# The last FFN by seven half products per pair of weight tiles (Strassen), with weight sums through PSUM and lo blocks split between VectorE and GpSimd

## The reference

```
def swiglu(h, w_in, w_out):
    gate, up = jnp.split(h @ w_in, 2, axis=-1)
    return (jax.nn.silu(gate) * up) @ w_out
# second_block, i = 1:
h = modulate(rmsnorm(x, norm_ffn_g[i]), sh2, sc2)
x = x + g2[:, None, :] * swiglu(h, w_ffn_in[i], w_ffn_out[i])
```

## Time and profile before

| | |
|---|---|
| median of three runs | 1659.35 us (1657.75 to 1660.1) |
| span of the profiled execution | 1656.0 us |
| TensorE busy in the span | 1628.9 us, 98% |
| VectorE, ScalarE, GpSimd busy | 804.0, 578.8, 734.7 us |
| last FFN (1281.5 to 1643 us) | 361.5 us |

### The profile page before, as it was taken

How to read it: one execution, slowest core, us unless ns; L and a number is a source line. 1 busy time by engine, 2 the same in 40 slices (tenths; PEclk the granted TensorE clock), 3 DMA queues, 4 the chain that set the end, 5 groups by cost and what they waited for, 6 DMA issues and landing times.

```text
span 1656.0 us, 21027 instructions
## 1 busy us (share of the span) xinstructions
PE 1628.9 (98%) x7254; PEld 1324.1 (80%) x7254; DVE 804.0 (49%) x1262; ACT 578.8 (35%) x790; POOL 734.7 (44%) x348
## 2 busy tenths in 40 slices
PE   8999999999999999999999999999999999999998
PEld 6785777878888888888888888888888888888886
DVE  6899887878565343433365161451725311111114
ACT  6434434344443322312244233232333431222233
POOL 5999133443244444444444334333424444444442
PEclk9999999999999999999999999999999999999999
DMA  9351266375455565555443223222213232222221
GB/s 383 119 208 65 90 239 212 115 263 206 179 204 190 203 253 192 199 195 187 159 148 107 69 89 101 67 85 78 98 52 96 82 101 94 96 99 92 95 74 61
DMA packets 65442, 233.71 MB, mean 141 GB/s; under 512 B 7264, under 2 KB 7264, under 8 KB 65120
## 3 DMA queue, kind: packets, MB, share of 16 engines
q1 hardware_dynamic: 65376, 232.82, 40.4%
HBM read 230.69 MB, written 2.10 MB: 141 GB/s over the span
## 4 chain that ended last, share of the span: by engine, by line
issue 55%; POOL 30%; PE 8%; DVE 3%; DMA 1%; ACT 1%; POOLq 1%; DVEq 0%; ACTq 0%
POOL w_lo L484 25%; POOL cv_acc L532 2%; PE bank L1542 2%; PE bank L1543 2%; PE bank L1544 2%; DVE mods_ring L1066 1%; POOL cv_y L514 1%; POOL diag L526 1%; POOL sq L526 1%; DVE x L1108 0%; DMA w_raw<-pl_v_in 0%; ACT sq L585 0%; DMA mods_ring<-w_mods_in 0%; PE bank L1573 0%; PE bank L1577 0%
## 5 line engine op out<-in xcount | busy, mean ns | idle before, releaser
L484 POOL TENSOR_TENSOR w_lo<-w_raw,w_hi 128x1024 fp32r<-128x1024 f32 x268 | 644.7, 2411 | 875.3 <-ACT w_hi L576 864.6
L1542 PE MATMUL bank<-h_hi,w_hi 128*128 128x512 f32 x1240 | 485.4, 391 | 1.2 <-POOL h_lo L496 0.9
L1544 PE MATMUL bank<-h_hi,w_lo 128*128 128x512 f32 x1240 | 482.7, 389 | 0.0
L1543 PE MATMUL bank<-h_lo,w_hi 128*128 128x512 f32 x1240 | 482.6, 389 | 0.0
L576 ACT ACTIVATE w_hi<-w_raw 128x1024 fp32r<-128x1024 f32 x264 | 277.8, 1052 | 261.1 <-PE bank L1544 242.8
L1542 PEld LDWEIGHTS bank<-h_hi,w_hi 128*128 128x128 f32 x1240 | 232.8, 188 | 51.7 <-issue 2.5
L1543 PEld LDWEIGHTS bank<-h_lo,w_hi 128*128 128x128 f32 x1240 | 232.8, 188 | 49.3 <-issue 1.2
L1544 PEld LDWEIGHTS bank<-h_hi,w_lo 128*128 128x128 f32 x1240 | 232.8, 188 | 48.5
L1542 PE MATMUL bank<-f_hi,w_hi 128*128 128x512 f32 x472 | 184.7, 391 | 0.9 <-DVE z_buf L1448 0.9
L1543 PE MATMUL bank<-f_lo,w_hi 128*128 128x512 f32 x472 | 185.0, 392 | 0.0
L1544 PE MATMUL bank<-f_hi,w_lo 128*128 128x512 f32 x472 | 183.6, 389 | 0.0
(11 more groups left out here) (271 smaller groups left out, 1847.6 us busy)
## 6 DMA issues: line engine op xcount, KB each, us to landing
mods_ring<-w_mods_in SPq DMA_DIRECT2D x152, 512.0 KB, 6.2
w_raw<-ff_in_in SPq DMA_DIRECT2D x88, 512.0 KB, 3.5
w_raw<-ret_in SPq DMA_DIRECT2D x64, 512.0 KB, 3.5
w_raw<-ff_out_in SPq DMA_DIRECT2D x32, 512.0 KB, 3.5
w_raw<-cv_ab_in SPq DMA_DIRECT2D x16, 512.0 KB, 6.3
w_raw<-ff_tail_in SPq DMA_DIRECT2D x16, 384.0 KB, 3.0
w_raw<-cv_g_in SPq DMA_DIRECT2D x8, 512.0 KB, 3.5
w_raw<-cv_out_in SPq DMA_DIRECT2D x8, 512.0 KB, 3.4
```

Source lines behind the costliest of these rows:

```text
L484: pool.tensor_tensor(w_lo[:, s, :], w_raw[:, s, :], w_hi[:, s, :].bitcast(F32), ALU.subtract).then_inc(lo_done, 1)
L1542: pe.matmul(out, w_h, m_h, start=start, stop=False)
L1543: pe.matmul(out, w_h, m_l, start=False, stop=False)
L1544: return pe.matmul(out, w_l, m_h, start=False, stop=stop)
```

## The change

The first four hidden chunks of the last FFN stay as they were (8 tiles, `in10`). All other tiles go in pairs (`PAIRS`, 30 of them: 18 up/gate pairs and 12 pairs of output tiles), each by the seven products of Strassen's method in Winograd's form. A pair's weights are two rows of tiles and are cut into four quarters of half the input chunks each: A11 and A12 (row 0, even and odd chunks), A21 and A22 (row 1). The host lays even chunks first. The moving side is cut into chunk parity and token halves of 256 (FRONT, BACK). The seven left blocks are, in TensorE's order, A11, S3 = A11 - A21, S1 = A21 + A22, A12, S2 = S1 - A11, A22, S4 = A12 - S2. A block has 4 chunks of 128 columns (3 in the last output pairs), and each takes three matmuls of 256 columns, so a pair takes 84 (63) where two tiles took 48 (36) of 512 columns.

- ScalarE copies A21 into PSUM (`ps_stat`), where VectorE makes S1 of it in place; S2 is in `ps_bc`, S4 in `c_all`, S3 in `diag` (SBUF). Each sum has one operand in PSUM. All seven blocks get a hi part by ScalarE (L1014), block j of the next pair when TensorE has left block j of this one. The lo parts of A11, S3, A12, A22 are GpSimd's (L570), those of S1, S2, S4 VectorE's (L1688).
- Four PSUM banks take the products. Those of an up/gate pair are put together by half copies on ScalarE (p1, p5, u2) and additions on VectorE (t7, c11, c22, c21, c12: up front, gate back, gate front, up back). ScalarE applies silu to c22 and c21, and VectorE multiplies. The next pair's blocks A11, A12, S3 and S1 start banks 0, 1, 2 and 3, which wait for c22, c11, c21 and c12. Output pairs are added to `x` straight from the banks.
- Each two finished chunks need four sums of token halves as further right sides, with hi parts by ScalarE and sums and lo parts by GpSimd. Before the first pair the same is made of `h`.
- SP loads a pair's two rows when GpSimd has made lo of A12 and A22 two pairs earlier. The first output pair of a part begins with the chunks that are ready.

The diff, cut to its core:

```diff
+LEFT_A11, LEFT_S3, LEFT_S1, LEFT_A12, LEFT_S2, LEFT_A22, LEFT_S4 = range(BLOCKS)
+LO_BY_POOL = (LEFT_A11, LEFT_S3, LEFT_A12, LEFT_A22)
+LO_BY_VECTOR = (LEFT_S1, LEFT_S2, LEFT_S4)
...
+PAIRS = [x for p, n in enumerate(PARTS)
+         for x in ([("in", p, c) for c in range(0 if p else STD_TILES // 2, n)]
+                   + [("out", p, m) for m in range(0, DC, 2)])]
+half_width = lambda q: PARTS[PAIRS[q][1]] // 2 * P if PAIRS[q][0] == "out" else 4 * P
...
+        c11, c12, c21, c22 = (over_h_lo[:, 2 * n, H:] for n in range(4))
+        s3_sum, s1_sum, s2_sum, s4_sum = diag[:], ps_stat[:], ps_bc[:], c_all[:, 0:T]
...
+                    if q < 2:
+                        sp.wait_ge(lo_done, U0["in10"] + STD_TILES - SLOTS + s + 1)
+                    else:
+                        sp.wait_ge(lo_by_pool, 4 * (q - 2) + 3 + row)
+                        sp.wait_ge(s_sum, 4 * (q - 2) + 4)
...
+            def half_lo_parts(q):
+                for j in LO_BY_POOL:
+                    pool.wait_ge(s_hi, BLOCKS * q + j + 1)
+                    pool.tensor_tensor(left_block(w_lo, q, j), left_raw(q, j), left_block(w_hi, q, j).bitcast(F32),
+                                       ALU.subtract).then_inc(lo_by_pool, 1)
...
+            def chunk_lo_and_t1(c):
...
+                pool.tensor_tensor(t13[:, FRONT], z_pair[0][:, BACK], z_pair[0][:, FRONT],
+                                   ALU.subtract).then_inc(t_sum, 1)
...
+            def chunk_lo_and_sums(c):
+                done, row = 4 * (c // 2), (c - 1) % 8
+                pool.wait_ge(z_made, c + 1)
+                pool.tensor_tensor(t13[:, BACK], z_pair[1][:, BACK], z_pair[0][:, BACK],
+                                   ALU.subtract).then_inc(t_sum, 1)
+                pool.wait_ge(t_sum, done + 2)
+                pool.tensor_tensor(t42[:, BACK], t13[:, BACK], z_pair[0][:, FRONT], ALU.add).then_inc(t_sum, 1)
+                pool.wait_ge(t_sum, done + 3)
+                pool.tensor_tensor(t42[:, FRONT], z_pair[1][:, FRONT], t42[:, BACK],
+                                   ALU.subtract).then_inc(t_sum, 1)
+                z_lo(row, slice(0, T), t13[:], ft_hi, ft_lo, done + 3)
+                z_lo(row + 1, slice(0, T), z_pair[1][:], f_hi, f_lo, done + 2)
+                z_lo(row + 1, slice(0, T), t42, ft_hi, ft_lo, done + 4)
...
+            for q, (kind, p, n) in enumerate(PAIRS):
+                c = chunk_made_before(q)
+                if c is not None and c % 2:
+                    chunk_lo_and_sums(c)
+                if q + 1 < len(PAIRS):
+                    half_lo_parts(q + 1)
+                if c is not None and c % 2 == 0:
+                    chunk_lo_and_t1(c)
...
+            def copy_a21(q):
...
+                if q:
+                    act.wait_ge(lo_by_vector, 3 * (q - 1) + 1)
+                act.activation(left_raw(q, LEFT_S1), raw_quarter(q, 1, 0), ACT.Copy).then_inc(a21_copied, 1)
...
+                        act.wait_ge(s_sum, 4 * q + {LEFT_S3: 1, LEFT_S1: 3, LEFT_S2: 4, LEFT_S4: 4}[j])
+                    if q:
+                        act.wait_ge(half_done, BLOCKS * (q - 1) + j + 1)
...
+                    act.activation(left_block(w_hi, q, j), left_raw(q, j), ACT.Copy).then_inc(s_hi, 1)
...
+                    if kind == "in":
+                        copy_half(q, LEFT_A11, 0, p1, 2)
+                        half_hi(q + 1, 0)
+                        if odd:
+                            sums_hi(c, 0)
+                        half_hi(q + 1, 1)
+                        if odd:
+                            sums_hi(c, 1)
+                        elif c is not None:
+                            chunk_hi(c)
+                        copy_half(q, LEFT_S1, 3, p5, 1)
+                        half_hi(q + 1, 2, 3)
+                        copy_a21(q + 2)
+                        copy_half(q, LEFT_S2, 0, u2, 5)
+                        half_hi(q + 1, 4)
+                        r = of_kind(q)
+                        if r:
+                            act.wait_ge(z_made, chunk_of(p, n))
+                        act.wait_ge(combined, 5 * r + 3)
+                        act.activation(gate_back, c22, ACT.Silu).then_inc(gated, 1)
+                        act.wait_ge(combined, 5 * r + 4)
+                        act.activation(gate_front, c21, ACT.Silu).then_inc(gated, 1)
+                        half_hi(q + 1, 5, 6)
+                        continue
+                    if odd:
+                        sums_hi(c, 0)
+                        sums_hi(c, 1)
+                    half_hi(q + 1, 0, 1, 2, 3)
...
+                        v.wait_ge(a21_copied, q + 1)
+                        if q:
+                            v.wait_ge(lo_by_pool, 4 * (q - 1) + 2)
+                        v.tensor_tensor(s3, a11, s1, ALU.subtract).then_inc(s_sum, 1)
+                    elif i == 1:
+                        v.wait_ge(s_sum, n + 1)
+                        v.tensor_tensor(s1, s1, a22, ALU.add).then_inc(s_sum, 1)
+                    elif i == 2:
+                        v.wait_ge(s_sum, n + 2)
+                        if q:
+                            v.wait_ge(lo_by_vector, 3 * (q - 1) + 2)
+                        v.tensor_tensor(s2, s1, a11, ALU.subtract).then_inc(s_sum, 1)
+                    else:
+                        v.wait_ge(s_sum, n + 3)
+                        if q:
+                            v.wait_ge(lo_by_vector, 3 * (q - 1) + 3)
...
+                    if kind == "in":
...
+                        half(LEFT_S1)
+                        v.wait_ge(copied, 3 * r + 2)
+                        if r:
+                            v.wait_ge(combined, 5 * (r - 1) + 3)
+                        v.tensor_tensor(t7, bank[2][:, 0:H], p5, ALU.add).then_inc(combined, 1)
+                        half_lo(q + 1, LEFT_S1)
+                        half(LEFT_A12)
+                        if r:
+                            v.wait_ge(z_made, chunk_of(p, n))
+                        v.tensor_tensor(c11, bank[1][:, 0:H], p1, ALU.add).then_inc(combined, 1)
+                        left_sum(q + 2, 0, 1)
+                        half(LEFT_S2)
+                        v.wait_ge(copied, 3 * r + 3)
+                        done(1)
+                        v.tensor_tensor(c22, bank[0][:, 0:H], t7, ALU.add).then_inc(combined, 1)
+                        half_lo(q + 1, LEFT_S2)
+                        left_sum(q + 2, 2)
+                        half(LEFT_A22)
+                        v.tensor_tensor(c21, bank[2][:, 0:H], u2, ALU.add).then_inc(combined, 1)
+                        half(LEFT_S4)
+                        v.tensor_tensor(c12, bank[3][:, 0:H], u2, ALU.add).then_inc(combined, 1)
+                        c = chunk_of(p, n)
+                        z = z_pair[c % 2]
+                        v.wait_ge(ft_lo_done, 4 * (c // 2))
+                        v.wait_ge(gated, 2 * r + 2)
+                        v.tensor_tensor(z[:, FRONT], c11, gate_front, ALU.mult)
+                        done(5)
+                        v.tensor_tensor(z[:, BACK], c12, gate_back, ALU.mult).then_inc(z_made, 1)
+                        half_lo(q + 1, LEFT_S4)
+                        left_sum(q + 2, 3)
+                        continue
+                    def update(c, cols, b, before=None):
...
+                    update(n + 1, BACK, 3, 2)
+                    half_lo(q + 1, LEFT_S1)
+                    half(LEFT_A12)
+                    update(n, FRONT, 1, 1)
+                    left_sum(q + 2, 0, 1)
+                    half(LEFT_S2)
+                    update(n, BACK, 0)
+                    v.wait_ge(x_part, 8 * r + 3)
+                    both = x[:, n + 1, :].rearrange("p (a n) -> p a n", a=2)
+                    u = bank[0][:, 0:H].rearrange("p (a n) -> p a n", a=1).to_broadcast([P, 2, H])
+                    v.scalar_tensor_tensor(both, u, gate(n5, n + 1), both, ALU.mult, ALU.add).then_inc(x_part, 1)
+                    half_lo(q + 1, LEFT_S2)
+                    left_sum(q + 2, 2)
+                    half(LEFT_A22)
+                    update(n + 1, FRONT, 2, 6)
+                    half(LEFT_S4)
+                    update(n, BACK, 3, 5)
+                    half_lo(q + 1, LEFT_S4)
+                    left_sum(q + 2, 3)
+                    if p == len(PARTS) - 1:
+                        if n == DC - 4:
...
+            HALF_BANK = {LEFT_A11: 0, LEFT_S3: 2, LEFT_S1: 3, LEFT_A12: 1, LEFT_S2: 0, LEFT_A22: 2, LEFT_S4: 3}
+            ALONE = (LEFT_A11, LEFT_S3, LEFT_S1, LEFT_A12)
...
+            def half_shares(q, j, chunks, of):
+                std_hi, std_lo, sums_hi, sums_lo = of
+                n = half_width(q) // P
+                for k in chunks:
+                    w = slice(k * P, (k + 1) * P)
+                    last = three(bank[HALF_BANK[j]][:, 0:H], left_block(w_hi, q, j)[:, w], left_block(w_lo, q, j)[:, w],
+                                 right(j, k, std_hi, sums_hi), right(j, k, std_lo, sums_lo),
```

(24 more changed lines are left out.)

320 lines of the change are left out of this document (295 added, 25 removed).

## The result

The changed kernel takes 1710.67 us (median of 4 runs, 1707.69 to 1716.17) against 1659.03 (4 runs); the ratio is 1.0317, 95% interval 1.0298 to 1.0336. It is slower by 51.6 us; 1707 was forecast. The profiled execution was the slowest of the four (1716.17, span 1714.4), so its stages add up to some 5 us more than the median shows.

What follows compares the result with a forecast made beforehand. It took TensorE alone to bound the kernel before, and in-order queues locking into each other to make the changed one slower: 1656.0 + 33.5 (stages) + 14 (clock) + 3.35 (span to median) = 1707 us, range 1666 to 1728.

Steps and rivals of the forecast that it cites:

- TensorE's pace: Half products in the last FFN: 256-column matmuls start every 0.118 us, an up/gate pair takes 9.91 us, 30.8 us saved without waits.
- The chain from Z: Up/gate pairs: from Z, GpSimd's start on a finished pair of chunks, in-order queues lock; next Z 26.0 us later.
- O: The up/gate pair of an odd chunk; TensorE was to start it at Z+10.6 and end it at Z+20.8.
- Where TensorE stands: TensorE stands 5.2 to 5.9 us before O in 6 places; E is the pair that makes an even chunk.
- The stages: Last FFN from the whole chunks through the pairs of parts 0 to 2: 395.4 us against 361.9, +33.5 us.
- The clock: Pauses before O in 6 places halve TensorE's granted clock: 6 x 2.4 = 14 us, lower bound 0, upper 20.
- Costed at nothing, the input sums on VectorE: First FFN input's sums (4 x about 4.5 us) lie beside 43.9 us of TensorE work, so cost nothing.
- Costed at nothing, the ends: After the last pairs: the ends of both kernels do the same, so they cost nothing.
- A: Rival for the pairs: no wait, all other engines stay under TensorE; 1629 us, chance 0.07.
- B: Rival for the up/gate pairs: the lag doesn't build up, two-pair cycle 22.3 us; 1664 us, give or take 7, chance 0.09.
- C: Rival: waits as forecast but the clock stays up; 1693 us, chance 0.28.
- D: The forecast itself: the queue waits in the last FFN plus the clock loss; 1707 us, chance 0.46.

Runs made afterwards that it cites:

- x2: Changed kernel with VectorE's weight sums for the pair after next moved behind the two products that make the chunk; 1670.86 us, ratio 1.0067 to the kernel before.
- x3: Changed kernel with GpSimd's lo blocks A11 and S3 of the next pair ahead of the three whole lo parts; 1688.10 us.
- x4: Changed kernel with ScalarE's hi part of block A22 of the next pair ahead of the two silus; 1687.01 us.
- x5: Changed kernel with extra 256-column matmuls filling TensorE's pauses in even-chunk pairs and first output pairs, output not the reference's; 1706.51 us.
- x9: x8 with 22 more zero-operand matmuls in TensorE's pause at each part's first output pair; 1658.52 us, ratio 0.9994 to the kernel before.
- x1: Changed kernel with VectorE's products of whole chunks 0 and 1 ahead of the input sums that stood before them; 1710.41 us.
- x8: Changed kernel with the edits of x2, x4 and x1 together; 1655.94 us, in a second set of runs 1656.86.

## Why the prediction was right, point by point

The direction, the time (1707 against 1710.67) and the mechanism were right. That the time is so close is luck in part: one term of the sum was much too large, and two that were costed at nothing made up for it.

- **TensorE's pace**: right. An undisturbed up/gate pair takes 9.75 us in the trace after (9.91 forecast). The figure of the Trainium skill ("TensorE: Matmul & The Clock Gate", Back-to-back issue gap), 0.109, was too low for these matmuls: they start 0.118 apart, 0.114 in some blocks.
- **The chain from Z**: right, step by step. Forecast and measured: lo of S3 Z+8.61 and 8.60, c22 done Z+10.46 and 10.48, TensorE starts O at Z+10.6 and 10.63, c21 Z+12.17 and 12.20, lo of A22 Z+14.5 and 14.5, copy of A21 Z+18.15 and 18.81, c22 of O started Z+20.2 and 20.93, next Z 26.0 and 26.8. The prices were sums of durations from the earlier trace rows. x2 and x3 show the S3 sum ahead of c22 and GpSimd's order to be causes, x4 the place of A22's hi. The raw buffer's part (0.9 us a cycle by the forecast) no run takes apart.
- **Where TensorE stands**: 3.6 us at O, where 5.2 to 5.9 were forecast, because 1.5 to 1.8 us stood before block A22 of E already (t7 behind ScalarE's p5, itself behind the hi parts that wait for GpSimd). The start of O is set by Z, so the sum didn't change.
- **The stages**: forecast without the clock, then measured, which includes it: part 0 pairs 47.8 and 49.1, output 46.6 and 48.2, part 1 97.1 and 101.9, output 46.6 and 48.1, part 2 71.1 and 74.6, last output 42.3 and 40.7 us. Together 351.5 and 362.5.
- **The clock**: the step that failed. The pauses do halve the granted clock, as the earlier trace rows show, and at the first output pairs too. But 6 x 2.4 = 14 us took nearly all of the slowed blocks as lost. For TensorE's own time that is about right (some 17 us, by x5's trace); the kernel lost 4.2 to 6.5 us by it (x5's runs; 8.8 by the stages of the two traces). The working had priced a local loss on an engine that didn't set the cycle. x9 agrees in part: a faster TensorE met the next wait sooner at the first place, but its extra matmuls also ran past the pause.
- **Costed at nothing, the input sums on VectorE**: wrong by 5.5 us of pause and some 2 of low clock in the first stretch (51.5 in place of 43.9); in four other traces of the same code it is 3.3 us of pause and 48.8 in all. The cover was real for VectorE's load but not for the order: TensorE waits for the product of chunk 1 at half of the stretch, and it stands behind sums of 2.13 and 2.67 us. The earlier trace rows had shown such an operation beside GpSimd, and the sums have two SBUF operands as well. The Trainium skill ("SBUF — State Buffer", SBUF: two separate sides) says that VectorE with two SBUF inputs and GpSimd exclude each other for whole instructions; the trace agrees (0.43 us alone, 2.13 beside GpSimd), and by it the price could have been set. x1 shows that it isn't simply added to the chain: with the pause gone, a wait for c22 took 3.1 us of it in the very next pair.
- **Costed at nothing, the ends**: wrong by 3.0 us (16.05 from TensorE's last weight matmul against 13.05). Both chunks of the last pair end together now, so the sum of squares of one is on the path, and the clock is low (0.72 in the last window):

```profile
1698.23 0.28 PE L1973 MATMUL bank<-f_hi,w_lo 128*128 128x256 f32 x1
1698.55 0.48 DVE L1781 SCALAR_TENSOR_TENSOR x<-bank,mod,x 128x256 f32<-128x256 f32 x1 [0.35 <-PE bank L1973]
1698.95 0.68 DVE L1275 TENSOR_TENSOR ssum<-c_all,sq 128x512 f32<-128x512 f32 x1
1699.67 0.42 ACT L1122 ACTIVATE sq<-x 128x256 f32<-128x256 f32 x1 [1.60 <-DVE ssum L1275]
1699.69 1.05 PE L2034 MATMUL ps_stat<-ones,ssum 128*128 128x1 f32 x8 [1.18 <-DVE ssum L1275]
```

- **The rivals**: A (1629) fell. B named A22's hi behind the silu as what decides, and x4 shows it to be half of that: 2.4 us a cycle, but 1687 us and not 1664, since the wait for c22 stays. C (the clock costs nothing, 1693) was nearer to the truth in mechanism than D; D's number was nearer by luck, through the terms that made up for it.

The rest of the difference between the profiled executions, 2.8 us, lies ahead of the last FFN, where no instruction changed; this start lies between 1281.4 and 1286.4 us in the traces of all the kernels here, so it is scatter.

## What to carry to other kernels

When engine queues are in order, put what frees a buffer for the busiest engine ahead of everything in its queue that prepares later work: three sums moved back in VectorE's queue were worth 40 us here, at equal load on every engine. A clock or pace loss on an engine that doesn't close the cycle is mostly covered (here 17 us of TensorE's time, 4 to 9 of the kernel's); write down the chain first and price losses on it alone. An experiment that fills a pause has to be checked for running past it. And "hidden beside x us of other work" must be checked against the next hand-over in that stretch, not against its whole length.

## What the runs showed of the hardware that was not expected

- 22 matmuls of 256 columns with a left operand of only 16 columns, all zeros, in the pause kept the granted clock at 1.00 behind it, where it had been 0.58 (x9 and the second set of x8; in the 6.8 us behind the other two pauses 1.00 and 0.75).
- Two 256-column sums with two SBUF operands on VectorE took 0.43 and 0.48 us alone, and 2.13 and 2.67 beside GpSimd's 128x1024 subtractions.
